# Four scale rows on TensorE, x loaded first, modulation before the second block's rounding: the opening of a two-block transformer kernel

## What is computed

```python
c_act = jax.nn.silu(c)
mod = c_act @ w_ada[l] + b_ada[l]
sh1, sc1, g1, sh2, sc2, g2 = [m[:, None, :] for m in jnp.split(mod, 6, axis=-1)]
h = _standardize(x) * (1.0 + sc1) + sh1
mix = _hybrid_mixer(h, w_in[l], ...)      # begins with proj = h @ w_in + b_in
```

## Time and profile before

| | us |
|---|---|
| median of 3 runs | 1599.56 |
| lowest and highest | 1599.09, 1600.26 |
| the profiled execution, its own time | 1600.27 |
| span of its trace | 1598.5 |
| PE busy in the span | 1575.9 (99%) |
| DVE, ACT, POOL busy | 756.5, 636.2, 681.6 |

### The profile page before, as it was taken

How to read it: one execution, slowest core, us unless ns; L and a number is a source line. 1 busy time by engine, 2 the same in 40 slices (tenths; PEclk the granted TensorE clock), 3 DMA queues, 4 the chain that set the end, 5 groups by cost and what they waited for, 6 DMA issues and landing times.

```text
span 1598.5 us, 19178 instructions
## 1 busy us (share of the span) xinstructions
PE 1575.9 (99%) x7560; PEld 1290.8 (81%) x7560; DVE 756.5 (47%) x1357; ACT 636.2 (40%) x1144; POOL 681.6 (43%) x518
## 2 busy tenths in 40 slices
PE   8999999999998999999999999999999999999998
PEld 6788867888897888888888887778878888888886
DVE  5999524656586352233317899742442421012103
ACT  3634563543435332233323325672452433224322
POOL 1585333244544444544456363004314444444542
PEclk7999999999999999999999999999999999999999
DMA  8676532268534363333333332002303333233331
GB/s 310 142 110 150 133 84 75 73 217 296 192 99 124 106 184 112 98 94 103 93 121 113 119 115 83 1 14 83 89 27 93 105 92 106 93 93 98 100 101 71
DMA packets 221706, 180.31 MB, mean 113 GB/s; under 512 B 24232, under 2 KB 184360, under 8 KB 221488
## 3 DMA queue, kind: packets, MB, share of 16 engines
q1 hardware_dynamic: 214512, 167.00, 36.1%
q10 hardware_dynamic: 7104, 12.08, 2.3%
HBM read 172.49 MB, written 6.55 MB: 112 GB/s over the span
## 4 chain that ended last, share of the span: by engine, by line
PE 77%; DVE 4%; ACT 2%; POOL 0%; issue 0%; DMA 0%; DVEq 0%; ACTq 0%
PE bank L631 13%; PE bank L637 13%; PE bank L632 13%; PE bank L713 9%; PE bank L718 9%; PE bank L714 9%; PE bank L758 2%; PE bank L1106 1%; PE bank L1077 1%; PE bank L741 1%; PE bank L743 1%; PE bank L742 1%; PE bank L1163 1%; PE bank L967 1%; PE bank L1149 0%; PE bank L1150 0%
## 5 line engine op out<-in xcount | busy, mean ns | idle before, releaser
L2483 POOL TENSOR_TENSOR w_lo<-raw,w_hi 128x512 fp32r<-128x512 f32 (+1 forms) x484 | 647.8, 1362 | 867.1 <-ACT w_hi L1233 866.3
L1233 ACT ACTIVATE w_hi<-raw 128x512 fp32r<-128x512 f32 (+1 forms) x484 | 276.0, 619 | 333.7 <-PE bank L718 256.0
L631 PE MATMUL bank<-h_hi,w_hi 128*128 128x512 f32 x936 | 367.1, 392 | 0.0
L632 PE MATMUL bank<-h_lo,w_hi 128*128 128x512 f32 x936 | 364.3, 389 | 0.0
L637 PE MATMUL bank<-h_hi,w_lo 128*128 128x512 f32 x936 | 250.3, 389 | 0.0
L631 PEld LDWEIGHTS bank<-h_hi,w_hi 128*128 128x128 f32 x936 | 175.8, 188 | 38.7 <-issue 2.4
L632 PEld LDWEIGHTS bank<-h_lo,w_hi 128*128 128x128 f32 x936 | 175.7, 188 | 36.6 <-issue 0.7
L637 PEld LDWEIGHTS bank<-h_hi,w_lo 128*128 128x128 f32 x936 | 175.7, 188 | 36.6
L2310 DVE SCALAR_TENSOR_TENSOR bank<-att_area,cols,bank 128x512 f32<-128x512 f32 x116 | 87.6, 755 | 3.9
L713 PE MATMUL bank<-w_hi,u_hi 128*128 128x512 f32 x224 | 87.1, 389 | 0.0
L714 PE MATMUL bank<-w_hi,u_lo 128*128 128x512 f32 x224 | 87.1, 389 | 0.0
(11 more groups left out here) (446 smaller groups left out, 2643.7 us busy)
## 6 DMA issues: line engine op xcount, KB each, us to landing
raw<-in_w_in SPq DMA_DIRECT2D x57, 512.0 KB, 4.4
raw<-in_w_ffn_up SPq DMA_DIRECT2D x44, 512.0 KB, 3.9
raw<-in_w_up SPq DMA_DIRECT2D x32, 512.0 KB, 4.0
raw<-in_w_down SPq DMA_DIRECT2D x32, 512.0 KB, 3.8
ada_ring<-in_w_ada SPq DMA_DIRECT2D x24, 512.0 KB, 5.7
raw<-in_w_ffn_down SPq DMA_DIRECT2D x20, 512.0 KB, 3.7
raw<-in_w_s_glu SPq DMA_DIRECT2D x16, 256.0 KB, 3.2
raw<-in_w_mlstm_down SPq DMA_DIRECT2D x8, 512.0 KB, 6.6
```

Of the source, the lines that this page charges most:

```text
L631: te.matmul(ps, wv[0][:, i, :], rh, start=(i == 0), stop=False)
L632: te.matmul(ps, wv[0][:, i, :], rl, start=False, stop=False)
L1233: sc.activation(W_HI[SLOT[key]][:, part_], raw[:, RAW_SLOT[key], part_], ACT.Copy).then_inc(*hi_set.up((key, n_)))
L2483: gp_.tensor_tensor(W_LO[s_][:, part_], raw[:, RAW_SLOT[key], part_], W_HI[s_][:, part_].bitcast(F32), ALU.subtract).then_inc(*lo_made.up( ...
```

## The change

Six things are changed.

1. `ADA_PE` becomes `((1, 3), (1, 3, 5, 7))`: of the scale, TensorE takes four row blocks and DVE four.
2. x is loaded ahead of the constants: ACT issues the constants on its own queue, and SP's list begins with x. DVE's four small operations on the constants (`half`) move behind the row statistics.
3. TensorE's order: turns 4 and 5 go between the row blocks 3, 5 and 7 of the scale; `other_columns(1)` follows without `keep_busy(4)`, which comes after it and writes bank 4, once `mod_set[0]` frees that bank; turns 6 and 7 go inside `feature_pair_high`, behind its steps i = 0 and i = 1.
4. `feature_pair_high` takes the bank of its second block only after the first block's first two matmuls.
5. ACT rounds only weight block 0 ahead of the modulation, block 1 behind column block f = 1, block 2 behind f = 7.
6. DVE makes the shift's columns behind row block 2 of the scale (before: behind row block 6).

```diff
-        ADA_PE = ((1, 3), (1,))
+        ADA_PE = ((1, 3), (1, 3, 5, 7))
...
-        def feature_pair_high(keys, hi, lo, ready, frees):
+        def feature_pair_high(keys, hi, lo, ready, frees, between):
 
             made = []
-            for key, free in zip(keys, frees):
-                ps = take("acc", key, free)
-                (wv,) = block(key, False)
-                made.append((key, ps, wv))
             for i in range(KD):
                 rh, rl = at(hi, lo, i)
                 pe.wait_ge(*ready[i])
-                for key, ps, wv in made:
+                for n, key in enumerate(keys):
+                    if i == 0:
+                        made.append((key, take("acc", key, frees[n]), block(key, False)[0]))
+                    _, ps, wv = made[n]
...
+                if i in between:
+                    between[i]()
...
-        def first_columns(part_):
+        def first_columns(part_, between={}):
...
+                for f in between.get(kk, ()):
+                    turn_h1(f)
...
-            first_columns(1)
-            turn_h1(4)
-            keep_busy(4)
+            first_columns(1, {3: (4,), 5: (5,)})
             other_columns(1)
-            turn_h1(5)
-            turn_h1(6)
-            turn["misc"] = 4
-            turn_h1(7)
+            pe.wait_ge(*mod_set[0])
+            keep_busy(4, 4)
+            h1_ready = [h1_lo[i] for i in range(KD)]
+
+            def last_turn():
+                turn["misc"] = 4
+                turn_h1(7)
+
+            feature_pair_high([("us", 0), ("us", 1)], h_hi, h_lo, h1_ready, [us_out[0], us_out[1]], {0: lambda: turn_h1(6), 1: last_turn})
             ring["misc"], turn["misc"] = [4, 5, 6, 7], 3
...
         def scalar():
+            for i, (dst, src) in enumerate(((cols[:, :], io["cols"]), (ident[:, :], io["ident"]), (iota, io["iota"][:, 0:NC]))):
+                sc.dma_start(dst, src).then_inc(*const_in.up(i))
...
-            high_to(2)
+            high_to(0)
             act.wait_ge(*mod_set[1])
             for f in range(KD):
                 modulated("h1", f, mod[:, KD + f:KD + f + 1], mod[:, f:f + 1], h1_sv, h1_dv, h1_hi)
+                if f == 1:
+                    high_to(1)
+            high_to(2)
...
-            dve.wait_ge(*const_in.all)
-            for i, nm in enumerate(("b_om", "b_ga", "b_gb", "mgain")):
-                ve.tensor_scalar(half[:, i, :], col(nm, 0, KD), 0.5, None, ALU.mult).then_inc(*half_set.up(i))
...
             row_inverse("x", 0, TT, 0, shift=True)
+            dve.wait_ge(*const_in.all)
+            for i, nm in enumerate(("b_om", "b_ga", "b_gb", "mgain")):
+                ve.tensor_scalar(half[:, i, :], col(nm, 0, KD), 0.5, None, ALU.mult).then_inc(*half_set.up(i))
...
-                    if (p_, kk) == (1, 6):
+                    if (p_, kk) == (1, 2):
                         ada_columns(0, 0, 0.0)
...
-            for i, (dst, nm) in enumerate(((cols, "cols"), (ident, "ident"))):
-                sy.dma_start(dst[:, :], io[nm]).then_inc(*const_in.up(i))
-            sy.dma_start(iota, io["iota"][:, 0:NC]).then_inc(*const_in.up(2))
```

More of the change, by code:

```diff
@@ L759, in transpose, with turn_h1 @@
             last.then_inc(*turned.up(key))
-        def first_columns(part_):
+        def turn_h1(f):
+            pe.wait_ge(*xn_set["x3"])
+            transpose(("h1", f), [xn1[:, t, f * P:(f + 1) * P] for t in range(TT)], h1_lo[f])
+        def first_columns(part_, between={}):
             ps = take("misc", ("ada", part_), mod_set[part_])
@@ L791, in tensor, with keep_busy @@
         def tensor():
-            def keep_busy(n):
+            def keep_busy(n, b=7):
                 for _ in range(n):
-                    te.matmul(bank[7][:, :], ones[:, :], scr[:, 2, :], start=True, stop=True)
+                    te.matmul(bank[b][:, :], ones[:, :], scr[:, 2, :], start=True, stop=True)
             pe.wait_ge(*ones_set.all)
@@ L801, in tensor @@
             ring["misc"], turn["misc"] = [4, 1, 2, 5, 6, 3, 0, 7], 7
-            def turn_h1(f):
-                pe.wait_ge(*xn_set["x3"])
-                transpose(("h1", f), [xn1[:, t, f * P:(f + 1) * P] for t in range(TT)], h1_lo[f])
             first_columns(0)
@@ L811, in tensor @@
             other_columns(0)
-            first_columns(1)
-            turn_h1(4)
-            keep_busy(4)
+            first_columns(1, {3: (4,), 5: (5,)})
             other_columns(1)
-            turn_h1(5)
-            turn_h1(6)
-            turn["misc"] = 4
-            turn_h1(7)
+            pe.wait_ge(*mod_set[0])
[5 more added lines that the diff above has]
+            feature_pair_high([("us", 0), ("us", 1)], h_hi, h_lo, h1_ready, [us_out[0], us_out[1]], {0: lambda: turn_h1(6), 1: last_turn})
             ring["misc"], turn["misc"] = [4, 5, 6, 7], 3
-            h1_ready = [h1_lo[i] for i in range(KD)]
-            feature_pair_high([("us", 0), ("us", 1)], h_hi, h_lo, h1_ready, [us_out[0], us_out[1]])
             pe.wait_ge(*s5_in.all)
```

## The result

The changed kernel takes 1607.78 us (median of 6 runs, 1605.20 to 1613.64) against 1599.91 for the kernel before beside it; the ratio is 1.0050, with an interval of 1.0039 to 1.0061. The forecast was 1609.5 us, slower. The profiled execution took 1605.20 us, the shortest of the six, so another profiled execution of the same kernel is read beside it. It comes from a second set of four runs, `e0_after_again`: median 1609.85 us (1608.82 to 1610.07), ratio 1.0058 (1.0045 to 1.0071); the profiled one took 1609.79. A median of 1607.8 had been expected, and row blocks of 3.4 us where they lie behind the fall of the clock, so more of them in any execution slower than 1605.2 us; the rival was that loads or DVE's sum make the difference, with row blocks that take the same.

What follows compares the result with a forecast made beforehand. The prediction took TensorE's own queue in the opening as the bound. First real matmul +9.0 us, turns 6 and 7 +0.9: 1599.56 + 9.9 = 1609.5 us, own range 1607.5 to 1611.5, whole range 1603.5 to 1613.0.

Steps and rivals of the forecast that it cites:

- What bounds the opening: Up to the scale's columns: TensorE's own queue, not DVE or the loads, ends the opening, at 38.8 us before the change.
- Loads: Start of the kernel: x and every piece of `w_ada` 0.9 us earlier, turns at 18.9 instead of 19.81; late constants covered.
- Row blocks 3, 5 and 7, and the columns, at the low clock: TensorE's scale work: three row blocks at 3.5 us each, 10.5 us, and `other_columns(1)` 3.5 us instead of 1.84.
- signs that the prediction named against itself: In the new trace: row blocks of 1.8 to 2.4 us each, or a TensorE gap after 60 us that absorbs the shift.
- Where the clock changes: Opening: clock up at 25.8 us, behind `keep_busy(2)`, and 0.50 from about 29 us until the last `keep_busy`.
- rival B: Opening: the clock holds some 3 us longer, about two row blocks run fast; +5, 1604.6 us; chance 0.13.
- The last keep_busy: `keep_busy(4, 4)` ahead of the first real matmul: 5.5 us, from 45.4 to 50.9, within bounds of 5.1 and 6.9.
- Turns 6 and 7 between products: Between real matmuls: eight transposes of about 0.117 us at the fast clock add 0.9 us.
- The sum: Whole shift: +9.0 us to the first real matmul and +0.9 for turns 6 and 7, +9.9 us.
- Nothing behind the opening takes it up: From 41.88 us on: TensorE's list is unchanged, so the opening's shift moves the kernel's end, with no place absorbing it.
- Rival A: Opening: the clock stays at 2.4 GHz through the row blocks; +0.1, 1599.7 us; chance 0.17.

Runs made afterwards that it cites:

- e0_after_again: The changed kernel again, nothing altered, a second set of four runs beside the kernel before: median 1609.85 us, ratio 1.0058.
- e2: The kernel before with four row blocks of the scale on TensorE and nothing else changed: 1609.34 us, ratio 1.0059.
- e1: The changed kernel with one row block of the scale on TensorE again, turns 4 and 5 behind it: 1601.61 us, ratio 1.0007.
- e7: The changed kernel without its last `keep_busy(4, 4)`: 1608.89 us, ratio 1.0054.
- e9: The changed kernel with ten useless 512-column matmuls from `other_columns(0)` on through the scale's row blocks, and two instead of four in the last `keep_busy`: 1611.23 us, ratio 1.0060.
- e8: The kernel before with x loaded first, and weight block 1 rounded behind f = 1, block 2 behind f = 7: 1600.57 us, ratio 0.9996.
- e0: Short for e0_after_again: the changed kernel run again unaltered, four runs, median 1609.85 us, ratio 1.0058.
- e5: The changed kernel with a useless 512-column matmul behind every fourth single-column matmul of the scale's row blocks, eight in all: 1612.43 us, ratio 1.0070.

## Why the prediction was right, point by point

- **What bounds the opening.** Right: TensorE's own queue, shown by e2 (the rows alone cost 0.59%) against e1 (the change without them 0.07%), and by DVE's wait of 9.88 us.
- **Loads.** 0.9 us was taken; the turns start at 18.54 instead of 19.81, 1.27 us earlier (of which only some 0.4 is left against e2, whose loads are those of before). The constants came late (ACT's first use at 9.27 us) and were covered as said.
- **Row blocks 3, 5 and 7, and the columns, at the low clock.** 3.5 us each was taken; from start to start it is 3.27 (33.18 to 36.45 in the second execution) and 3.41 for the columns. Right in kind and within 0.25 us in size, but in the first execution for row blocks 5 and 7 alone: row block 3 ran fast there, one of the signs that the prediction named against itself (row blocks of 1.8 to 2.4 us).
- **Where the clock changes.** The mis-sized step. I carried the rise at 25.8 us over from the trace of before; it came at 22.6 in the profiled execution, so that `keep_busy(2)` took 2.0 us and not 3.4 and two row blocks ran fast until the fall at 29.4, and at 24.4 in the second, with the fall at 27.9 (29.2 before). The columns end at 40.94 and 44.02 us, where I had 45.4. The first execution (1605.2 us) is the case of rival B (1604.6), which I gave 0.13; the second (1609.8) is the forecast (1609.5); the median of six lies between them. That it fell into the forecast's own range (1607.5 to 1611.5, by 0.28 us) is in part luck: it lies between two cases, and the forecast priced one of them. Rival B's terms were also added up wrongly: 9.9 less 3.4 and at most 1 is +5.5 to +6.5 us, not +5; measured were +6.1 up to L697.
- **The last keep_busy.** 5.5 us was taken, 5.85 and 5.25 measured. That it gives back about what it costs (e7) was not in the working.
- **Turns 6 and 7 between products.** +0.9 us was taken; 46.79 to 55.40 is 8.61 us, against 7.39 before: +1.2.
- **The sum.** +9.9 us was forecast up to L696 (L697 after); +6.1 measured in the first execution, +8.6 in the second. The medians differ by 7.9.
- **Nothing behind the opening takes it up.** Right for the changed kernel with one exception that is the clock's: of the 6.1 us the span of the first execution shows 4.9. TensorE's wait near 490 us is as long as before (4.62 against 4.50 us), but the low clock behind it is shorter, and the 32 transposes there take 5.02 instead of 6.33 us:

```profile
494.28 5.02 PE L759 MATMUL bank<-ident,branch 128*128 128x128 f32 x32 [4.62 <-ACT branch L1253]
```

  In the second execution they take 6.22, and its span is 9.5 us longer than the earlier trace rows where 8.6 stand at L697; 0.3 of the 0.9 is this wait (4.79 us), the rest is not traced. And "no place behind it" was too broad: DVE's S5 chain is a place where a shift can grow. TensorE turns for 1.91 us before it needs what ACT copies behind the chain, and in e9 it goes on 0.78 us after the chain's end. So by an estimate from these the chain of the kernel before may come 104.97 + 1.91 - 0.78 - 103.23 = 2.9 us later against TensorE before it stalls. In e9 it came 5.3 us later (11.68 against 6.39), and 5.3 less 2.9 is the wait of 2.4.
- **Rival A, the clock up through all row blocks.** It would have brought a time near 1600 us. The stretch from 30 to 41 us of the changed kernel, busy for all 11.00 us at 0.50, says otherwise for single-column products, and e9 shows that the same products do run at 1.00 with matmuls of 512 columns among them (0.95 us for eight, 33 to 36 us at 1.00).

## What to carry to other kernels

A free engine is not free if its queue is the path: count the records that a moved piece of work adds to the engine that everything waits for, and price them at the clock they will find. Here a record of a single-column product took 0.11 us at a granted clock of 1.00 and 0.21 at 0.50 (1.84 and 3.41 us for 16), and runs of them without a gap did not keep the clock up (0.50 from 30 to 41 us). Before work is taken off an engine, ask in the trace who waits for it: here DVE had been done for 2.7 us when TensorE got to its sum.

## What the runs showed of the hardware

- Two levels of the clock: in all fourteen profiled executions every stretch of half a microsecond from 1 to 58 us has a granted clock of 0.50 or 1.00, save those in which it changes. The profile gives no frequency. An estimate from e8: at 0.50 its products of 512 columns start 0.426 us apart (ten from 38.44 to 42.70 us), 1.20 columns per ns, which is 1.2 GHz if a column takes one cycle, and 2.4 GHz would be twice that. At 1.00 they start 0.227 us apart (sixteen from 49.27 to 52.90 us in the kernel before), 2.25 columns per ns.
- Single-column products and their weight loads: the 32 records from 25.71 us in the changed kernel keep PE busy for 3.71 us and have 32 weight loads of 128x128 beside them, which keep PEld busy for 3.65. A transpose moves 128 columns, and its record took about as long: 0.22 us at 0.50 (four from 30.24 to 31.12 in the kernel before), where one of a single column took 0.20 to 0.21 (16 in 3.27 and in 3.41 us from start to start). What sets the price was not tested.
- The clock's rise and fall did not lie at fixed times from the start. Within the same `keep_busy(2)` it rose at 25.8 us in the kernel before, at 22.6 and 24.4 in two executions of the changed kernel. They differ before anything that was changed on TensorE: the sixteen records of `keep_busy(8)`, from 1.55 us in every kernel here, took 8.51 to 10.13 us in the fourteen profiled executions. Work whose price hangs on that may spread the times: the changed kernel's six single runs lie 8.4 us apart, the six of the kernel before beside it 2.3; but the changed kernel's four in e0 lie 1.3 apart and 26 of the kernel before 4.6, so how much more it spreads is not settled. Between the two executions of the changed kernel the rise differs by 1.8 us.
- In e9, with useless matmuls that began while the clock was up, it stayed at 1.00 from 24 to 45 us. In e5, with the same kind of matmuls begun after it had fallen, it was 0.50 from 27 to 39 us and rose at 40.3. Each is one execution, so what the single runs without a profile did is not shown.
- In the 32 transposes near 490 us, which follow a wait and start at 0.50, the clock rose while they ran, at 493.4 us in the kernel before and at 497.0 and 502.3 in the two executions of the changed kernel. In the sixteen of the opening (19.81 to 23.28 us in the kernel before) it was 0.50 throughout.
- A stall of TensorE cost more than its own length in e9: 2.4 us of waiting brought 1.6 us of slow transposes behind it (3.47 us for 16, where 32 take 3.65). In e5 a stall of 0.40 us at the same place did not (2.04 us for 16).
- Steps of DVE took 1.0 to 1.1 us longer when they ran beside POOL's rounding of weights: 0.16 us in the kernel before and 1.28 in e9 for one, 2.55 and 3.65 for another. What lies behind it was not tested.
